# Two-layer encoder with top-2 experts on one core: the order of rounds, gathers and products back in a layer's first expert items

## What is computed

```python
def reference(x, norm1_g, w_in, ...):
    for l in range(DEPTH):
        x = x + mixer_sublayer(x, norm1_g[l], w_in[l], ...)
        x = x + hier_moe(rms_norm(x, norm2_g[l]), w_router_group[l], ...)
    return x

def hier_moe(h, w_rg, b_rg, w_re, b_re, w_gate, w_up, w_down):
    ...  # top-1 of 4 groups, then top-2 of its 8 experts, gates by softmax
    def expert_block(args):
        e, idx = args
        xb = xt[idx]
        return (jax.nn.silu(xb @ w_gate[e]) * (xb @ w_up[e])) @ w_down[e]
    ...  # each token gets the weighted sum of its two experts
```

## Time and profile before

| what | value |
|---|---|
| median of 3 runs | 1155.28 us (1154.23 to 1157.55) |
| the profiled execution | 1156.21 us, its span 1154.4 us |
| TensorE matmul busy | 985.6 us, 85% of the span, 5,408 instructions |
| TensorE weight loads busy | 463.4 us, 40% |
| VectorE busy | 291.4 us, 25% |
| ScalarE busy | 178.2 us, 15% |
| DMA | 437.07 MB, 379 GB/s on the mean |
| mean granted clock | 0.931 |

### The profile page before, as it was taken

One profiled execution on the slowest core, in us unless ns is written; L12 is line 12 of the kernel. 1 busy time (PEld: TensorE's weight loads), 2 busy tenths in 40 slices (PEclk: granted clock), 3 DMA queues, 4 the chain that ended last, 5 costly groups with the idle time before them and its releaser, 6 DMA issues.

```text
span 1154.4 us, 13601 instructions
## 1 busy us (share of the span) xinstructions
PE 985.6 (85%) x5408; PEld 463.4 (40%) x5408; DVE 291.4 (25%) x796; ACT 178.2 (15%) x444; POOL 51.6 (4%) x104
## 2 busy tenths in 40 slices
PE   9999999998887946648999999999969779474687
PEld 5556644453343412113356656444524234131242
DVE  4546552111110110001145555421111101100011
ACT  1344311110010000001024333111100001000110
POOL 2121100000000000000021111000000000000000
PEclk9999999999898987769999999999989889687799
DMA  9962889999999999999998248999999999999997
GB/s 317 350 253 110 360 313 418 426 429 426 426 429 427 426 430 426 427 429 419 399 396 314 97 182 332 364 406 427 428 426 428 428 426 428 427 429 428 427 418 294
DMA packets 61879, 437.07 MB, mean 379 GB/s; under 512 B 10910, under 2 KB 15350, under 8 KB 31350
## 3 DMA queue, kind: packets, MB, share of 16 engines
q1 hardware_dynamic: 61813, 436.17, 92.0%
HBM read 435.10 MB, written 1.44 MB: 378 GB/s over the span
## 4 chain that ended last, share of the span: by engine, by line
PE 63%; DMA 31%; DVE 3%; SPq 1%; issue 1%; POOL 1%; ACT 0%; DVEq 0%; POOLq 0%
PE bank L1076 31%; DMA ring<-in_w_down 16%; DMA ring<-in_w_gate 10%; PE bank L785 9%; PE bank L1102 5%; DMA ring<-in_w_up 5%; PE bank L917 5%; PE bank L1030 4%; PE bank L744 1%; PE bank L863 1%; PE bank L853 1%; SPq L515 1%; PE bank L885 1%; PE bank L1094 1%; PE bank L876 1%
## 5 line engine op out<-in xcount | busy, mean ns | idle before, releaser
L1076 PE MATMUL bank<-ring,work 128*32 128x512 f32 (+2 forms) x2608 | 484.4, 666 | 132.5 <-DMA ring<-in_w_up 51.0
L1076 PEld LDWEIGHTS bank<-ring,work 128*32 128x32 f32 (+2 forms) x2608 | 146.5, 131 | 396.4 <-issue 393.7
L785 PE MATMUL bank<-ring,hT 128*128 128x512 f32 (+1 forms) x384 | 128.2, 488 | 0.8 <-DVE hT L1431 0.8
L785 PEld LDWEIGHTS bank<-ring,hT 128*128 128x128 f32 x384 | 71.3, 190 | 48.1 <-issue 42.4
L1030 PEld LDWEIGHTS bank<-work,h 128*128 128x128 f32 x704 | 82.3, 192 | 16.5 <-issue 15.6
L1030 PE MATMUL bank<-work,h 128*128 128x128 f32 x704 | 86.8, 277 | 1.6 <-DVE work L1796 1.6
L1076 PE MATMUL bank<-work 128*32 128x512 f32 (+2 forms) x176 | 75.0, 617 | 12.0 <-DMA ring<-in_w_down 12.0
L1102 PE MATMUL bank<-work 128*128 128x512 f32 x176 | 81.4, 603 | 2.4 <-ACT work L1384 1.6
L1076 PE MATMUL bank<-kept,work 128*32 128x512 f32 (+1 forms) x160 | 75.4, 624 | 7.4 <-DMA ring<-in_w_up 7.4
L1852 DVE COPY work<-bank 128x512 f32<-128x512 f32 x20 | 13.8, 691 | 240.4 <-PE bank L1076 240.4
L1847 DVE TENSOR_TENSOR work<-work,bank 128x512 f32<-128x512 f32 x22 | 15.1, 687 | 223.5 <-PE bank L1076 223.5
(11 more groups left out here) (212 smaller groups left out, 702.3 us busy)
## 6 DMA issues: line engine op xcount, KB each, us to landing
ring<-in_w_gate SPq DMA_DIRECT2D x42, 2048.0 KB, 25.9
ring<-in_w_down SPq DMA_DIRECT2D x38, 2048.0 KB, 23.8
ring<-in_w_up SPq DMA_DIRECT2D x36, 2048.0 KB, 29.4
ring<-in_w_up SPq DMA_DIRECT2D x36, 1024.0 KB, 14.7
ring<-in_w_down SPq DMA_DIRECT2D x28, 1024.0 KB, 10.3
ring<-in_w_gate SPq DMA_DIRECT2D x20, 1024.0 KB, 9.1
ring<-in_w_in SPq DMA_DIRECT2D x8, 1536.0 KB, 13.5
ring<-in_w_out SPq DMA_DIRECT2D x8, 1024.0 KB, 17.1
```

Source lines behind the costliest of these rows:

```text
L785: last = matmul(bank[6 + i % 2][:, 0:c1 - c0], hT[:, k, t * P:t * P + P], group_in(l, gi)[:, k, c0:c1], start=(k == 0), stop=(k == KD - 1))
L1076: last = nc.tensor.matmul(bank[b][e * w:e * w + w, :], lhs[:, k, e * w:e * w + w], rows(pos, k_count // 2)[:, kk, n * 512:n * 512 + 512], ...
```

## The change

In item 0 of each layer the rounds run in the order gate0, up0, gate1, up1 (`FIRST_ORDER`; the plan's waits follow it). Its gather is cut into four quarters of two chunks, one bank each (`gather_first`): two quarters ahead of gate0, two behind up0. DVE copies quarters 0, 1 and 3, ACT quarter 2; the new counts `p_first` and `v_first` tie them. Items 1 and 2 are gathered in their second half (`gather_high`) behind down1 of the item before, not ahead of down0. And `back` of items 0 and 1 stands behind gate0 of the next item (`LATE_BACK`).

```diff
--- before.py
+++ after.py
@@ -99,6 +99,10 @@
 
 
 HALVED = {(l, *key): 3 * l + n for l in range(LAYERS) for key, n in (((1, 5, 1), 1), ((2, 0, 0), 2), ((2, 0, 1), 2), ((2, 0, 2), 3), ((2, 0, 3), 3))}
+FIRST_ORDER = (0, 2, 1, 3, 4, 5)
 
 
 def whole(i, r):
@@ -137,11 +141,12 @@
         for i, it in enumerate(TIME):
             q = l * NI + i
             for r, name in enumerate(ROUNDS):
-                done = ("p_down", 2 * q + 2) if r == 5 else ("p_round", 5 * q + r + 1)
+                n = FIRST_ORDER.index(r) if i == 0 else r
+                done = ("p_down", 2 * q + 2) if r == 5 else ("p_round", 5 * q + n + 1)
                 for e in range(KINDS[it]):
                     allowed = [EARLY] if i == r == e == 0 else everything if i <= BESIDE_LAST else ring
                     if not whole(i, r):
-                        take((l, i, r, e), 1, done, t0 + 100 + 10 * i + r, allowed)
+                        take((l, i, r, e), 1, done, t0 + 100 + 10 * i + n, allowed)
                     elif r % 2 == 0:
                         done = ("p_down", 2 * q + 2) if r == 4 else ("p_round", 5 * q + r + 2)
                         take((l, i, r, e), 2, done, t0 + 100 + 10 * i + r + 1, allowed)
@@ -322,6 +327,8 @@
             sem("v_" + n) for n in ("router", "chosen", "flags", "order", "step"))
         v_pick, v_pickw, v_xg, v_hid, v_y, v_istep = (sem("v_" + n) for n in ("pick", "pickw", "xg", "hid", "y", "istep"))
         v_back = [sem(f"v_back{n}") for n in range(4)]
+        p_first, v_first = sem("p_first"), sem("v_first")
         g_init, g_rstd, g_step, g_rope, g_route = (sem("g_" + n) for n in ("init", "rstd", "step", "rope", "route"))
 
         d_again = sem("d_again")
@@ -378,6 +385,8 @@
         BACK = [(0, 0), (1, 0), (0, 1), (1, 1)]
 
         SUM0 = 2
+        LATE_BACK = 2
 
         def pair(i):
             return ((6, 7), (0, 1))[i % 2]
@@ -1050,9 +1059,19 @@
                 gather_low(i, q)
                 gather_high(i, q)
 
+            def gather_first(half):
+                for n in (2 * half, 2 * half + 1):
+                    for k in range(2):
+                        for t in range(TT):
+                            last = matmul(bank[n][:, k * P:k * P + P], x_kc[:, t, 2 * n + k, :], pick[:, t, :],
+                                          start=(t == 0), stop=(t == TT - 1))
+                    last.then_inc(p_gather if n % 2 else p_first, 1)
             def first(l):
                 pe.wait_ge(a_rows, TT * (l + 1))
-                gather(0, l * NI)
+                pe.wait_ge(v_pick, l * NI + 1)
+                gather_first(0)
 
             hidc = hid.rearrange("p (f c) -> p c f", c=KE)
 
@@ -1071,6 +1090,12 @@
                     for n, b in enumerate(banks):
                         for kk in range(k_count // 2):
                             k = r % 2 * k_count // 2 + kk
+                            if i == 0 and r < 2 and kk == 2:
+                                if r == 0:
+                                    pe.wait_ge(v_xg, q + 1)
+                                else:
+                                    pe.wait_ge(v_first, 2 * l + 2)
                             for e in range(n_e):
                                 pos = PLAN[l, i, r, e][0]
                                 last = nc.tensor.matmul(bank[b][e * w:e * w + w, :], lhs[:, k, e * w:e * w + w],
@@ -1096,17 +1121,29 @@
                     if kk == 1:
                         last.then_inc(p_down, 1)
 
-                def back(ns):
+                def back(ns, of=i):
                     for n in ns:
                         t, half = BACK[n]
                         last = nc.tensor.matmul(bank[SUM0 + n][:, :], pickT[:, t, :], y[:, half * 512:half * 512 + 512],
-                                                start=(i == 0), stop=(i == NI - 1))
+                                                start=(of == 0), stop=(of == NI - 1))
                         last.then_inc(p_back, 1)
 
                 if i == NI - 1:
                     gather(i, q)
-                pe.wait_ge(v_xg, q + 1)
+                if i == 0:
+                    pe.wait_ge(v_first, 2 * l + 1)
+                else:
+                    pe.wait_ge(v_xg, q + 1)
                 round_of(0, (b0,), xg, p_round)
+                if i == 0:
+                    round_of(2, (b1,), xg, p_round)
+                    gather_first(1)
+                if 0 < i <= LATE_BACK:
+                    pe.wait_ge(a_pickT, q)
+                    pe.wait_ge(a_y, q)
+                    pe.wait_ge(v_y, q)
+                    back(range(4), i - 1)
                 if i == NI - 1:
                     warm(other[0], 5)
                 pe.wait_ge(a_xg, q + 1)
@@ -1125,7 +1162,8 @@
                     biases(l + 1, 0, other[1])
                     pe.wait_ge(v_gains, l + 2)
                     biases(l + 1, 1, other[0])
-                round_of(2, (b1,), xg, p_round)
+                if i:
+                    round_of(2, (b1,), xg, p_round)
                 if i == NI - 1 and l < LAYERS - 1:
                     for hd in range(2, 4):
                         pe.wait_ge(v_rel, 4 * l + 4 + hd - 1)
@@ -1142,7 +1180,7 @@
                 for c in range(KE):
                     last = nc.tensor.transpose(bank[b0][:, c * P:c * P + P], hidc[:, c, :], ident[:])
                 last.then_inc(p_hidT, 1)
-                if i < NI - 2:
+                if 2 <= i < NI - 2:
                     gather_high(i + 1, q + 1)
                 pe.wait_ge(a_hidT, q + 1)
                 round_of(4, (b0, b1), hidT, p_round)
@@ -1150,6 +1188,10 @@
                     round_of(5, (b0, b1), hidT, p_down)
                 else:
                     lower_rows(0, (0, 1))
+                if i < 2:
+                    gather_high(i + 1, q + 1)
+                if i < LATE_BACK:
+                    return
                 pe.wait_ge(a_pickT, q + 1)
                 pe.wait_ge(a_y, q + 1)
                 back((0, 1))
@@ -1365,7 +1407,10 @@
                 last.then_inc(a_xg, 1)
 
             def first(l):
-                gathered(0, l * NI)
+                act.wait_ge(p_first, 2 * l + 2)
+                for k in range(4, 6):
+                    last = nc.scalar.mul(xg[:, k, :], bank[2][:, (k - 4) * P:(k - 3) * P], gain2[:, l, k:k + 1])
+                last.then_inc(a_xg, 1)
 
             def item(l, i, q):
                 b0, b1 = pair(i)
@@ -1373,15 +1418,17 @@
                     gathered(i, q)
                 act.wait_ge(p_pickT, q + 1)
                 nc.scalar.copy(pickT.rearrange("p t s -> p (t s)"), bank[pair(i + 1)[1]][:, 0:2 * P]).then_inc(a_pickT, 1)
-                act.wait_ge(p_round, 5 * q + 2)
+                act.wait_ge(p_round, 5 * q + (3 if i == 0 else 2))
                 nc.scalar.activation(hid, bank[b0][:, :], ACT.Silu).then_inc(a_silu, 1)
                 act.wait_ge(p_hidT, q + 1)
                 nc.scalar.copy(hidT.rearrange("p c s -> p (c s)"), bank[b0][:, :]).then_inc(a_hidT, 1)
-                if i < NI - 2:
+                if 2 <= i < NI - 2:
                     act.wait_ge(p_round, 5 * q + 4)
                     gathered(i + 1, q + 1)
                 act.wait_ge(p_down, 2 * q + 1)
                 nc.scalar.copy(y[:, 0:512], bank[b0][:, :]).then_inc(a_y, 1)
+                if i < 2:
+                    gathered(i + 1, q + 1)
                 if i == NI - 2:
                     rows_back(l)
 
@@ -1781,6 +1828,11 @@
                 dve.wait_ge(p_gather, 2 * q + 1)
                 tt(xg[:, 0:4, :], bank[pair(i)[0]][:, :].rearrange("p (k s) -> p k s", k=4), wide(gain2[:, q // NI, 0:4], P), ALU.mult).then_inc(v_xg, 1)
 
+            def copy_quarter(l, n, done):
+                tt(xg[:, 2 * n:2 * n + 2, :], bank[n][:, 0:2 * P].rearrange("p (k s) -> p k s", k=2),
+                   wide(gain2[:, l, 2 * n:2 * n + 2], P), ALU.mult).then_inc(done, 1)
             half_of = [slice(e * P // 2, (e + 1) * P // 2) for e in range(2)]
 
             def first(l):
@@ -1798,8 +1850,11 @@
                 last.then_inc(v_pick, 1)
                 expert_order(l)
                 placings(l)
+                dve.wait_ge(p_first, 2 * l + 1)
+                copy_quarter(l, 0, v_first)
+                dve.wait_ge(p_gather, 2 * q + 1)
+                copy_quarter(l, 1, v_xg)
                 expert_order_rest(l)
-                copy_gathered(0, q)
                 gates(l)
                 seated(nc.vector.tensor_copy(rgc[:, TT:], rg[:, TT:, e0:e0 + 2]))
                 dve.wait_ge(p_round, 5 * q + 1)
@@ -1808,6 +1863,8 @@
                         last = ts(pickw[:, t, half_of[e]], iota[:, 1:P // 2 + 1], rgc[:, t, e:e + 1], rgc[:, TT + t, e:e + 1],
                                   ALU.is_equal, ALU.mult)
                 last.then_inc(v_pickw, 1)
+                dve.wait_ge(p_gather, 2 * q + 2)
+                copy_quarter(l, 3, v_first)
                 seatings(l)
 
             weights = col[:, 10:12, :].rearrange("p c t -> p (c t)")
```

## The result

The changed kernel took 1158.8 us (median of 20 runs, 1156.97 to 1163.05) beside 1156.02 us for the kernel before, timed in the same comparison. Ratio 1.0021, 95% interval 1.0014 to 1.0028: slower by 2.4 us (1.6 to 3.2). A second comparison later gave 1.0013 (1.0005 to 1.0022), 1.5 us. A few launches, of whichever kernel, took far longer (1219 to 5580 us) and stand in no ratio. The forecast was +1.2 us, "same" by the bound of 0.3%; 0.21% is within that bound and 1158.8 us within the range of 1152.2 to 1159.6, but the cost is twice the one forecast. The step that sets it, a tighter release at gate1 of item 1, is in the trace. Lines of the changed kernel: L1067 `gather_first`, L1101 rounds, L1039 the other gathers, L1127 `back`, L1181 the transposes of the hidden rows.

The account below looks back on a forecast made before the run. Weight transfers at about 426 GB/s bound the kernel, so early DMA idle is paid at layer end. The tightest release moves from 153.0 to 153.55, some +0.6 us a layer, +1.2 on 1155.28: 1156.5 us, range 1152.2 to 1159.6.

Parts of the forecast that it names:

- The bound: Weight transfers from about 205 us run at 426 GB/s until layer end, so earlier DMA idle time is paid there.
- The early start: Item 0: gate0 starts at 145.4 instead of 147.26, so the first four releases come 1.8 us earlier; later releases swallow this.
- the first stretch: 147 to 161 us in layer 0: 6.4 us lost before (6.8 in layer 1), forecast to fall under 5.5.
- the second: 161 to 205 us in layer 0: 1.8 us lost before (2.3 in layer 1), forecast to rise over 3.
- Rival 1: The early start of the loads is kept in both layers: -3.7 us, 1151.6 us; chance 0.12.
- The vector queue behind the new wait: Item 0: vector copies quarter 3 at 154.35, delaying seatings and picks; TensorE waits 0.8 us, down0 starts about 166.1.
- Rival 2: The vector engine's quarter-3 wait does not bite: -0.75 us a layer, -1.5 us in all, 1153.8 us; chance 0.16.
- The largest release: Release time less load time asked for ahead: the maximum moves from item 1's gate0 (153.0) to its gate1 (153.55).
- The size: Difference of the largest release values, 153.55 - 153.0: +0.55, taken as some +0.6 us a layer, +1.2 in all.
- Rival 3: Item 1's gate1 was already as tight as gate0, so its 2.0 us delay passes whole: +4.0 us, 1159.3; chance 0.17.
- the scheme: Each round's release time T minus 2.46 us per piece asked for ahead; the largest sets the whole stream's push-back.
- 153.0: Release time less load time at item 1's gate0 in the kernel before: 180.1 with 11 pieces ahead, the largest there.

Follow-up runs that it names:

- order and quarters alone: Changed kernel with the other gathers and products back returned to their old places, against the kernel before: ratio 1.0006.
- with the late pick taken away: Only item 0's new round order and quartered gather, quarter 3 copied by the scalar engine, against the kernel before: 1.0004.
- the split: Products back in pairs behind the next item's gate0 and gate1: 0.9993 on the kernel before, 0.9991 on the changed kernel with quarter 3 on scalar; both against the kernel before.
- products back early: Changed kernel with the products back ahead of the next item's gate0, as before the change, against the kernel before: 1.0038, 4.4 us slower.

## Why the prediction was right, and what it mis-sized

- **The bound.** Right. From 205 us to 570 all kernels run at 425 to 426 GB/s, and what they differ by is lost ahead of that.
- **The early start is swallowed.** Right, and shown. At the same distance from the gather the first stretch lost 1.2 and 1.7 us less, the second 2.4 us more, which leaves +1.2 and +0.7 (the stream has +1.1 and +0.8 in the two layers); order and quarters alone gained nothing in time, and 0.4 us a layer at most in the trace with the late pick taken away. The sign named for it, a first loss under 5.5 us, was missed by 0.2 us in layer 0 and met in layer 1 (5.0); the second loss, over 3, was met in both. Rival 1 is out, and with it the rule of the Trainium skill ("Perfetto Trace Analysis", Optimization Strategy) as I had applied it: the long gap was shortened by making what ends it start sooner, and the runs show no time for it (1.0006 and 1.0004). A gap on the most contended resource is worth closing only as far as the next release allows.
- **The vector queue behind the new wait.** Right in place and size: copy at 155.04 less 0.53 = 154.5 (forecast 154.35), pick wait 0.62 us (0.8), hid wait 0.16 us, hidT copy uncovered 0.68 us (0.65). The copy itself is short; what delays the seatings is the wait ahead of it: they begin at 154.9 instead of 151.86, and of these 3.1 us about one reaches down0. Moving one copy away gave back 0.85 to 1.05 us a layer. Rival 2 is out: the wait bites.
- **The largest release moves to item 1's gate1.** Right: the split helps only where the new order makes gate1 the largest.
- **The size.** Forecast 0.6 us a layer, the trace 0.75 to 0.95. The step that was short is gate1's end: 185.55 forecast, 186.13 measured. 0.2 us came from down0's start (the transposes behind the wait for hid took 0.77 us where I had used 0.48, and hid came a little sooner than forecast), 0.2 from the moved gather, which took 1.98 us where I had used 1.79 (1.79 is what it took behind the transposes, 1.98 what each half gather of a later item behind a round takes in the chain), and the rest from 3.58 and 7.09 us for rounds behind a gather or a wait, where I had used 3.51 and 7.02. With 186.1 the value is 154.1, +1.1 a layer; the time says +0.75 to +1.2. So the mechanism and the place were right, and the term that was too small is gate1's shift, 2.6 us where I had 2.0.
- **Rival 3**, +4.0 us, gate1's shift passing whole: out by the timed intervals, and by the split on the old order.
- **What the scheme overprices.** Wherever a gate0 was the largest value it came out too high: +1.2 for +0.8, +0.3 for -0.4, +0.9 to +1.7 for +0.3, +3.3 for +1.8. Where down0 or gate1 was, it was within 0.4. The kernel before is itself one of the gate0 cases, but its 153.0 does not look far off: the kernels whose largest value was not a gate0 came out within 0.3 us a layer of their forecast against it, some above and some below. Why gate0's releases cost less than their value was not found.

## What to carry to other kernels

Where loads wait for places in a ring, price an edit by every release behind it, each as its time less the load time of all that is asked for ahead of it: the largest sets how far the stream is pushed back, and starting sooner than that only makes the queue wait later. Before a copy is put ahead of a queue of work on another engine, look who else could do it; a 0.42 us copy on the vector engine that first had to wait cost 0.85 to 1.05 us a layer, and on the scalar engine, which was idle then, it left the stream where it was before the change (-0.1). Work that fills the gap behind a short copy is cover, and moving it away shows the copy.

## What the runs showed that was not expected

- Four products that take 3.63 us in one place cost 0.7 us a layer more in the stream than two and two where the round behind them was the tightest; in the old order of item 0 the split made no difference (-0.7 against -0.75).
- A queue that has run silent comes back over some 2 us. In the kernel with order and quarters alone the loads behind item 0's down0 were issued at 171.57 us; the next two stretches of 2 us:

```profile
171.88:173.88 2.00, 2.00 (x12) 0.66 (x10) 0.00 (x0) 0.59 (x1) 0.00 (x0) 1.00 0.67 123
173.88:175.88 2.00, 2.00 (x9) 0.71 (x6) 0.69 (x1) 0.00 (x0) 0.00 (x0) 1.00 1.00 422
```

  123 GB/s in the first, 422 in the second. The changed kernel is alike: loads issued at 170.63 us, then 143 and 422 GB/s in the two stretches of 2 us from 170.94 on; so is the one with products back early, at 181.86 us: 147 and 406. So far as these show, the delay is the same from kernel to kernel, and it cancels in a difference.
- The first gather of layer 0 started between 142.9 and 144.8 us from kernel to kernel with nothing changed ahead of it. That is as much as the largest effect here, so stretches are to be compared from the gather's start on.
